# V as the stationary side for two heads in two attention kinds, and more products of constants in two waits

## The reference

```python
h = rmsnorm(x, ln1_g[i]) @ w_in[i]
o_fox  = fox_group(...)    # 4 heads of 64: causal, bias cum[q] - cum[k]
o_diff = diff_group(...)   # 4 heads, two softmaxes each, V of 128, o1 - lam*o2, rmsnorm
o_mla  = mla_group(...)    # 4 heads, q and k of 96, V of 64, chunk mask
x = x + jnp.concatenate([o_fox, o_diff, o_mla], -1) @ w_o[i]
# each head: softmax(q k^T + bias) @ v, in query blocks of 128
```

## Time and profile before

| | us |
|---|---|
| median of 3 runs | 2642.71 (2642.2 to 2642.84) |
| profiled execution | 2641.86 |
| its span | 2640.4 |
| TensorE matmul busy | 2567.4 (97%) |
| VectorE busy | 1157.4 (44%) |
| ScalarE busy | 896.9 (34%) |

### The profile page before, as it was taken

How to read it: one execution, slowest core, us unless ns; L and a number is a source line. 1 busy time by engine, 2 the same in 40 slices (tenths; PEclk the granted TensorE clock), 3 DMA queues, 4 the chain that set the end, 5 groups by cost and what they waited for, 6 DMA issues and landing times.

```text
span 2640.4 us, 32796 instructions
## 1 busy us (share of the span) xinstructions
PE 2567.4 (97%) x13272; PEld 1783.5 (68%) x13276; DVE 1157.4 (44%) x2170; ACT 896.9 (34%) x1715; POOL 354.0 (13%) x162
## 2 busy tenths in 40 slices
PE   8999999999999999999999999999999999999999
PEld 6875444444777444444477688888888767888887
DVE  3543322332686222332265433562554644465264
ACT  4431111111483111111164554442345445443233
POOL 2200000000341000000031011222222001123212
PEclk9999999999999999999999999999999999999999
DMA  6229999999423999999932012323131212223212
GB/s 216 67 92 419 419 420 419 420 419 419 154 96 132 419 419 419 420 419 419 419 128 80 33 64 66 110 86 106 64 116 51 80 49 65 64 96 113 87 63 81
DMA packets 139033, 543.26 MB, mean 206 GB/s; under 512 B 18816, under 2 KB 30336, under 8 KB 89728
## 3 DMA queue, kind: packets, MB, share of 16 engines
q1 hardware_dynamic: 129264, 536.94, 52.1%
q10 hardware_dynamic: 9616, 4.18, 0.6%
HBM read 538.99 MB, written 2.10 MB: 205 GB/s over the span
## 4 chain that ended last, share of the span: by engine, by line
PE 92%; DVE 5%; ACT 2%; issue 1%; POOL 0%; DMA 0%; ACTq 0%; POOLq 0%; DVEq 0%
PE ps L615 24%; PE ps L1413 17%; PE ps L617 15%; PE ps L1435 9%; PE ps L1388 5%; PE ps L637 5%; PE ps L549 3%; PE ps L1450 3%; PE ps L1451 2%; PE ps L2017 2%; PE ps L1986 2%; PE ps L550 1%; PE ps L2008 1%; DVE AT L2202 1%; PE ps L467 1%
## 5 line engine op out<-in xcount | busy, mean ns | idle before, releaser
L615 PE MATMUL ps<-w,w 128*128 128x512 f32 x2976 | 678.9, 390 | 2.6 <-POOL w L279 2.6
L615 PEld LDWEIGHTS ps<-w,w 128*128 128x128 f32 x2976 | 557.9, 188 | 119.6 <-POOL w L279 3.4
L279 POOL TENSOR_TENSOR w<-w,w 128x1024 fp32r<-128x1024 f32 (+2 forms) x136 | 329.9, 2434 | 2153.4 <-ACT w L271 2149.1
L1413 PE MATMUL ps<-w,w 128*64 128x512 f32 x2048 | 451.6, 594 | 1.8 <-issue 1.8
L617 PE MATMUL ps<-w,w 128*128 128x512 f32 (+1 forms) x1872 | 408.1, 379 | 3.2 <-DVE w L535 3.0
L271 ACT ACTIVATE w<-w 128x1024 fp32r<-128x1024 f32 (+2 forms) x260 | 252.8, 999 | 416.3 <-PE ps L617 183.4
L617 PEld LDWEIGHTS ps<-w,w 128*128 128x128 f32 x1872 | 337.9, 188 | 69.8 <-issue 4.7
L279 DVE TENSOR_TENSOR w<-w,w 128x1024 fp32r<-128x1024 f32 (+2 forms) x124 | 202.3, 1638 | 385.3 <-ACT w L271 382.7
L1413 PEld LDWEIGHTS ps<-w,w 128*64 128x64 f32 x2048 | 146.0, 137 | 285.5 <-issue 285.5
L1674 DVE TENSOR_TENSOR X<-ps,X 128x512 f32<-128x512 f32 x256 | 162.4, 682 | 181.7 <-PE ps L1451 180.7
L1435 PE MATMUL ps<-w,w 128*64 128x512 f32 x1024 | 226.8, 595 | 0.8 <-ACT w L1502 0.8
(11 more groups left out here) (252 smaller groups left out, 2283.6 us busy)
## 6 DMA issues: line engine op xcount, KB each, us to landing
w<-in_moe_w_gate SPq DMA_DIRECT2D x128, 1024.0 KB, 16.2
w<-in_moe_w_up SPq DMA_DIRECT2D x128, 1024.0 KB, 18.5
w<-in_moe_w_down SPq DMA_DIRECT2D x128, 1024.0 KB, 15.5
w<-in_w_up SPq DMA_DIRECT2D x40, 1024.0 KB, 5.1
w<-in_w_down SPq DMA_DIRECT2D x20, 1024.0 KB, 5.1
w<-in_w_in SPq DMA_DIRECT2D x16, 1024.0 KB, 5.3
w<-in_ab_w_in SPq DMA_DIRECT2D x10, 1024.0 KB, 5.2
w<-in_c_w_in SPq DMA_DIRECT2D x8, 1024.0 KB, 6.1
```

What stands on the lines that cost most here:

```text
L279: up(self.wlo[self.low[s][0]], lane.e.tensor_tensor(lo, raw, hi.bitcast(F32), ALU.subtract))
L615: ins = pe.matmul(bank[:, :], wp[:, k, P * o:P * o + P], ap(k0 + k), start=first, stop=stop)
L1413: ins = pe.matmul(bank[64 * e:64 * e + 64, :], XG[p % 3][:, 4 * u + k, 64 * e:64 * e + 64], w[e][:, k, :], start=(u == 0 and k == 0), stop ...
```

## The change

mla now pairs heads in a step, as fox did. In mla and fox, VectorE multiplies the probabilities in PB by the reciprocal row sum before they are turned (`vector_scaled`, signal `scaled`, on which the turn waits). `tensor_values` takes V (128 keys x 64) as stationary side and the turned probabilities (128 columns) as moving side, head e of the pair into partitions 64e to 64e+63 of one bank, so that the bank holds O transposed for two heads. For fox this is a block of a feature: ScalarE copies it as high part (`scalar_fox_features`), VectorE subtracts for the low part. For mla, VectorE copies it to O, and the high and low parts are made ahead of fox's step 4, from SBUF. The transposes of features 0, 1, 6 and 7 go. Nine products of constants stand ahead of step 2 of the first pipeline, and 36 instead of 18 behind the second layer of experts.

```diff
-            tensor_busy(10 if next_norm else 18)
+            tensor_busy(10 if next_norm else 36)
...
-    FEATURES_OUT = (6, 7, 4, 5, 2, 3, 0, 1)
+    FEATURES_OUT = (4, 5, 2, 3)
...
-                     lambda j, h=h: VM[:, j, 64 * h:64 * h + 64], 64) for h in range(4) for qc in BLOCKS]
+                     lambda j, h=h: VM[:, j, 64 * h:64 * h + 64], 64)
+                    for two in range(2) for qc in BLOCKS for h in (2 * two, 2 * two + 1)]
...
+            pipeline(mla_jobs + diff_jobs, 0, engine, {2: first, M_DIFF // 2 + 2: dv, n: fqk}, range(n + 4))
...
+            at_step = {2: fv, 4: mla_feature}
+            for n in range(2):
+                at_step[5 + n] = lambda n=n: o_feature(FEATURES_OUT[2 * n:2 * n + 2])
...
         def tensor_values(m, two):
-            for m, (qc, _, _, _, _, vals, dv) in turned_jobs(m, two):
-                n = turn_of(m)
-                PE.wait_ge(bpt.free, n + 1)
-                bank = banks.take(bo)
-                for j in range(qc + 1):
-                    ins = pe.matmul(bank[:, 0:dv], PTB[n % 4][:, P * j:P * j + P], vals(j), start=(j == 0), stop=(j == qc))
-                up(bo.full, ins)
+            bank = banks.take(bo)
+            qc, kind, _, _, _, vals, dv = two[0]
+            PE.wait_ge(bpt.free, turn_of(m + 1) + 1)
+            for j in range(qc + 1):
+                if kind == "diff0":
...
+                else:
+                    for e in range(2):
+                        ins = pe.matmul(bank[64 * e:64 * e + 64, 0:P], two[e][5](j), PTB[turn_of(m + e) % 4][:, P * j:P * j + P],
+                                        start=(j == 0), stop=(j == qc))
+            up(bo.full, ins)
...
-                    PE.wait_ge(bo.free, N_TURNS)
-                    tensor_o_features(FEATURES_OUT[6:])
...
+                    PE.wait_ge(bo.free, N_STEPS - 4 + 4 * k)
...
+        def scalar_fox_features(m, two):
+            qc, kind, h = two[0][:3]
+            if kind == "fox":
+                S.wait_ge(bo.full, m // 2 + 1)
+                up(fox_hi, act.activation(HTH[:, h // 2, P * qc:P * qc + P], bo.banks[bo.full.base + m // 2][:, 0:P], ACT.Copy))
...
+        def scalar_mla_features():
+            S.wait_ge(bo.free, M_DIFF // 2)
+            for k in (6, 7):
+                up(mla_hi, act.activation(by_chunk(HTH[:, k, :]), mla_values(k), ACT.Copy))
...
-            engine = (2, scalar_turn), (0, scalar_scores), (squares_lag, scalar_squares_of_values)
+            engine = (2, scalar_turn), (0, scalar_scores), (3, scalar_fox_features), (squares_lag, scalar_squares_of_values)
...
+        def vector_scaled(m, two):
+            if two[0][1] != "diff0":
+                vector_reciprocals(m)
+                V.wait_ge(rc, m // 2 + 1)
+                n = P * (two[0][0] + 1)
+                for m in (m, m + 1):
+                    up(scaled, dve.tensor_scalar(PB[m % 4][:, 0:n], PB[m % 4][:, 0:n], AT[:, 16 + m % 8:17 + m % 8], None, ALU.mult))
...
         def vector_values(m, two):
...
+            elif kind == "mla":
+                up(bo.free, dve.tensor_copy(O[:, qc, 768 + 64 * h:768 + 64 * h + P], bank[:, 0:P]))
+            else:
+                V.wait_ge(fox_hi, (m - M_FOX) // 2 + 1)
+                at_qc = slice(P * qc, P * qc + P)
+                up(bo.free, dve.tensor_tensor(HTL[:, h // 2, at_qc], bank[:, 0:P], f32(HTH[:, h // 2, at_qc]), ALU.subtract))
...
-            engine = (2, vector_mixture), (0, vector_scores), (sums_lag, vector_reciprocals), (values_lag, vector_values), (1, vector_share)
+            engine = (2, vector_scaled), (2, vector_mixture), (0, vector_scores), (1, vector_sums), (values_lag, vector_values), (1, vector_share)
```

More of the change, by code:

```diff
@@ L1943, in turn_of, with values_before @@
             return M_DIFF + (m - M_DIFF) // 2 if m < M_FOX else m - len(diff_jobs) // 2
+        def values_before(turn):
+            if turn < M_DIFF:
+                return turn // 2 + 1
+            return turn - M_DIFF // 2 + 1 if turn < turn_of(M_FOX) else (turn + len(diff_jobs) // 2) // 2 + 1
         def turned_jobs(m, two):
@@ L1959, in pipeline, with two_kinds, third_kind @@
                             part(m0 + m, jobs[m:m + 2])
-        def two_kinds(engine, dv, fqk):
+        def two_kinds(engine, dv, fqk, first=lambda: None):
             n = M_FOX // 2
[L1965 to L1971, removed]
+            pipeline(mla_jobs + diff_jobs, 0, engine, {2: first, M_DIFF // 2 + 2: dv, n: fqk}, range(n + 4))
+        def third_kind(engine, fv, mla_feature, o_feature):
+            at_step = {2: fv, 4: mla_feature}
+            for n in range(2):
+                at_step[5 + n] = lambda n=n: o_feature(FEATURES_OUT[2 * n:2 * n + 2])
             pipeline(fox_jobs, M_FOX, engine, at_step, range(len(fox_jobs) // 2))
@@ L2004, in tensor_turn @@
                 else:
-                    PE.wait_ge(bsc.free, m + 1)
+                    PE.wait_ge(scaled, (m if m < M_DIFF else m - len(diff_jobs)) + 1)
                 bank = banks.take(bpt)
@@ L2025, in tensor_o_feature, with nothing @@
             tensor_o_features(ks)
+        def nothing():
+            pass
         def tensor():
@@ L2202, in vector_scores, with vector_reciprocals @@
                 up(mx, dve.tensor_reduce(AT[:, m % 8:m % 8 + 1], bank[:, 0:n], AX, ALU.max, negate=True))
-        def vector_reciprocals(m, two):
+        def vector_reciprocals(m):
             V.wait_ge(bsc.free, m + 2)
@@ L2235, in vector_values, with vector_mla_features @@
         def vector_values(m, two):
-            for m, (qc, kind, h, _, _, _, dv) in turned_jobs(m, two):
-                bank = bo.next(V)
+            bank = bo.next(V)
+            qc, kind, h, _, _, _, dv = two[0]
+            if kind == "diff0":
                 V.wait_ge(rc, m // 2 + 1)
-                c0 = 256 + P * h if kind == "diff0" else (768 if kind == "mla" else 0) + 64 * h
-                up(bo.free, dve.tensor_scalar(O[:, qc, c0:c0 + dv], bank[:, 0:dv], AT[:, 16 + m % 8:17 + m % 8], None, ALU.mult))
+                up(bo.free, dve.tensor_scalar(O[:, qc, 256 + P * h:256 + P * h + dv], bank[:, 0:dv], AT[:, 16 + m % 8:17 + m % 8],
+                                              None, ALU.mult))
+            elif kind == "mla":
+                up(bo.free, dve.tensor_copy(O[:, qc, 768 + 64 * h:768 + 64 * h + P], bank[:, 0:P]))
+            else:
+                V.wait_ge(fox_hi, (m - M_FOX) // 2 + 1)
+                at_qc = slice(P * qc, P * qc + P)
+                up(bo.free, dve.tensor_tensor(HTL[:, h // 2, at_qc], bank[:, 0:P], f32(HTH[:, h // 2, at_qc]), ALU.subtract))
+        def vector_mla_features():
+            for k in (6, 7):
+                V.wait_ge(mla_hi, k - 5)
+                up(mla_lo, dve.tensor_tensor(by_chunk(HTL[:, k, :]), mla_values(k), by_chunk(f32(HTH[:, k, :])), ALU.subtract))
         def vector_o_features(ks):
```

38 lines of the change are left out of this document (23 added, 15 removed).

## The result

The change made the kernel slower by 5.5 us.

| | before | after |
|---|---|---|
| median (18 runs each) | 2643.13 (2641.95 to 2644.52) | 2648.68 (2647.25 to 2650.41) |
| ratio, 95% interval | | 1.0020 [1.0013, 1.0027] |
| span of the profiled execution | 2640.4 | 2647.1 |
| VectorE busy | 1157.4 | 1169.5 |

The account below looks back on a forecast made before the run. TensorE was 92% of the chain, but a VectorE and ScalarE loop was taken to bound fox. Mla -2.7, fox +4.1, rest -2.1 make -0.7 a layer, -1.4 in all: 2641.3 us, own range 2636 to 2646, 8 in 10 within 2627 to 2651.

Parts of the forecast that it names:

- Values: Value products in mla and fox: two records run side by side, 0.107 us a pair, 2.34 less in four steps.
- Rival C: Value products at 128 columns: pairs not side by side, 11.1 us more in all, 2652.4 us; chance 0.07.
- Bare loads (D): Value products in mla and fox's rest: each pair also pays its load, 5.2 us in all, 2646.5 or 2646.7; chance 0.05.
- Scaling: New VectorE work on mla and fox probabilities: reciprocal and scalings take 3.2 us in four steps, bounds 1.4 and 4.0.
- Mla: Steps 0 to 9 up to diff's V: 2.7 us less a layer, steady four steps 10.9 us for 11.46.
- The start: Mla's first steps: constants fill TensorE's wait, the slow clock goes; net 1.2 us less, plus 0.2 from steps 0 to 3.
- Values of step 10: Values after mla: 0.35 us less, which diff's own waits take back, so nothing gained.
- Fox: Steps 2 to 7: scaling and block copy lengthen the loop between maxima, 14.41 to 18.9 us; +4.1 us a layer.
- The rest: Fox's rest, first turn to last piece of w_o: 6.23 us becomes 4.1, 2.1 us less a layer.
- Behind the experts: 36 products of constants: transposes at full clock, first product still waits for low parts; nothing, at worst 1.6 us once.
- rival B: Clock falls in fox's new waits: three a layer at some 1.6 us each, 9.8 in all, 2651 us; chance 0.12.
- Rival A: TensorE stays the bound in fox, which loses 3.2 us; 8 us less a layer, 2626.7 us; chance 0.22.

Follow-up runs that it names:

- experiment 1: Changed kernel with products of constants filling fox's waits in steps 4, 5 and 7: 2643.27 us, ratio 0.9999 to the kernel before.
- experiment 4: Changed kernel without the nine products of constants in mla's first wait: 2653.75 us, ratio 1.0036 to the kernel before.
- experiment 6: Changed kernel with mla's features moved behind fox's step 7, features 2 and 3 behind fox's rest: 2637.56 us, ratio 0.9984 to before.
- experiment 10: experiment 6 (subtraction still at lag 3) with features 4 and 5 ahead of fox's step 3 instead of 5: 2643.21 us, ratio 1.0003 to before.
- experiment 12: experiment 9 with VectorE's low parts of features 4 and 5 ahead of step 4 instead of step 3: 2626.58 us, ratio 0.9943 to before.
- experiment 5: Changed kernel with 18 products of constants behind the experts instead of 36: 2648.83 us, ratio 1.0018 to before.
- experiment 9: experiment 10 with VectorE's subtraction for a fox block one step later (lag 4 instead of 3): 2633.55 us, ratio 0.9964 to before.
- experiment 8: Changed kernel with only VectorE's subtraction for a fox block one step later (lag 4): 2642.55 us, ratio 1.0003 to before.

## Why the prediction was wrong

The steps in the order of the prediction:

- **Values, right.** 0.107 us a pair at 128 moving columns (16, 12, 8 and 4 records in 1.09, 0.88, 0.66 and 0.44 us). Rival C is out: pairs run side by side.
- **Bare loads (D), out.** By the Trainium skill, "TensorE: Matmul & The Clock Gate", section "Part 3: Packing small matmuls — row/col tiling", loads on the same rows as a matmul in flight would not overlap; the same section makes an exception for a load into the background weight buffer, which the prediction left out. The trace has 16 such loads, 0.85 us, within the 1.09 us of their products: it does not agree with the bare rule at 128 columns either, and whether the exception is what it shows no run tells. (The prediction gives D two times, 2646.5 and 2646.7; its 5.2 us over the forecast make 2646.5.)
- **Scaling, nearly right in length.** Reciprocal to end of the scaling: 0.67, 0.81, 0.94 and 1.07 us for one to four blocks, 3.5 in four steps for 3.2.
- **Mla, right.** 21.52 us for 21.2 up to diff's first scores, clock 1.00. The steady state, from step 4 to diff's first scores, is 10.92 us for the 10.9 of the sum, 0.62 less than before. The start gave 1.07 (step 4 starts 10.60 us after step 0, before 11.67) where the sum had 1.4, although the nine products alone are worth 1.33; the two steps behind gave 0.76 for 0.7. Together -2.45 for -2.7. "Values of step 10: nothing" was wrong by a little: 0.34 stayed gained.
- **Fox, the loop right, the clock wrong.** The intervals of 5.1, 5.2, 4.8 and 3.8 came as 4.56, 5.15, 4.79 and 3.84 where the clock held (experiment 1), and the stage as 23.54, +4.07 for +4.1. That it agrees so closely is partly luck: the first interval is 0.5 shorter than forecast, and what lies around the maxima 0.5 longer. The waits of TensorE were there, ended by the scaling as said: 1.18, 1.74, 0.75, 1.72 for 1.8, 1.8, 1.1, 1.75. In the kernel after it took 25.90.
- **The rest, right.** 4.05 us for 4.1; the last turn waits 1.17 for the scaling.
- **Behind the experts, right in the time.** Nothing gained or lost: 14.36 us from the last product of the experts to the first of the projections, before and after. "The transposes then run at full clock" did not come in the profiled execution (3.46 us for 1.86), and cost nothing.
- **The step that failed** is the choice between the forecast and rival B. The prediction computed waits of 1.75 to 1.8 us, saw a fall behind one of 2.46, and took its sum at a clock of 1.00, giving B 0.12. There was no row of a shorter wait in a stage as thin as this (TensorE busy 20 of 26 us, nearly all of it short products), and its absence was read as evidence of none. B's mechanism happened: two falls a layer, not three (1.18 and 0.75 kept the clock), 1.45 us each with what hangs over into the piece, 5.8 in all for B's 9.8 (three of 1.6 in two layers would be 9.6). But B's condition, a length of wait that is enough in this stage, is not shown: waits of the same length kept the clock in experiments 4, 6 and 10. Forecast and these falls make 2641.3 + 5.8 = 2647.1; 2648.68 was measured, and the one fall at 2050 in the profile is 1.6 of it.
- **Rival A was wrong for this order and right for another.** Its arithmetic gave fox 19.47 - 3.2 = 16.3 us. In experiment 12, with features and subtractions elsewhere in the order, TensorE is busy for 15.21 us, and the transposes of features 2 and 3, moved behind, are 0.97 more: 16.2. That TensorE's work of this stage is so short was right, and VectorE's order kept the gain from arriving. The 15 us of experiment 12 are near A's 16, but they are those of another order and contain luck with the clock.

## What to carry to other kernels

Work moved from the full engine to one at 44% is free only if its place in that engine's order lets it be. Sum the loop (maximum, exp, copy, low part, scaling). Put first on VectorE what TensorE waits for, and later what only frees a bank, asking who takes that bank.

When a prediction computes new waits of 1.7 us among short products, put the price of the clock's falls into the sum with a chance of its own, not into a rival at 0.12: here 10 of 18 such waits were followed by one. Filling the wait with products of constants shows in one run what the falls cost. In the kernel after, filling gave back 5.4 us of the loss; reordering the work so that the waits went gave 15 us against before.

## What was not expected of the hardware

The same wait in the same instructions can lose the clock or keep it. The turns of fox wait 1.71 to 1.74 us in five of the profiled executions:

| kernel | such waits, two layers | followed by a fall |
|---|---|---|
| after | 4 | 4 |
| experiment 5 | 4 | 4 |
| experiment 4 | 4 | 2 |
| experiment 6 | 4 | 0 |
| experiment 10 | 2 | 0 |

The waits of 2.46 to 2.68 us (mla's start before and in experiment 4, fox's step 3 in experiments 9 and 10) were followed by a fall in all eight cases. In the kernel after, 1.18 and 0.75 were not, nor was the 1.02 of experiment 12. What stands around a wait might count: the 1.74 had a wait of 1.18 one step ahead in the kernel after and none in experiment 6. It doesn't decide either, since experiment 4 had the 1.17 and kept the clock behind its 1.73, and in experiment 8 one layer lost the clock and the other did not, with the same instructions. What decides stays open.

The clock can also fall without any wait. In the projections there is a stretch of 20 products of 4 columns. In the kernel after it went well in the first layer and not in the second, where the columns behind it ran at 1.2 GHz:

```profile
1404.00:1407.40 3.40, 3.40 (x17) 2.79 (x16) 2.99 (x24) 0.00 (x0) 0.00 (x0) 1.00 1.04 402
2050.30:2053.70 3.40, 3.40 (x10) 2.62 (x9) 2.99 (x25) 0.00 (x0) 0.00 (x0) 0.50 1.04 401
```

```profile
2047.79 2.29 PE L2065 MATMUL ps<-sb_cum,CT 128*128 128x4 f32 x20
2049.94 2.58 PE L615 MATMUL ps<-w,w 128*128 128x512 f32 x6
```

There it costs 1.6 us by the starts of the products around it, in the first layer 1.0 (from the first product of the projections to mla's first scores 83.95 us in experiment 1, which has it, and 82.90 after). In the profiled executions of the fourteen kernels it happened never (before, experiments 8 and 12), once or twice. Whether the change makes it likelier is open; it is as large as some of the terms above, and a single profile can't tell them apart.
